# Where each half of the next weight tile is split, from step 28 on: at the step's beginning, or behind the attention operations of its first two gaps

## The chip, the cores and the metric

The kernel runs on one core of a Trainium2 chip. The metric is the time of one execution on the device in microseconds (us). Of the kernel before there are three runs, 1799.41 to 1800.14 us, with a median of 1799.8 us.

## What is computed

One layer of a hybrid backbone, in float32, for 128 context tokens and 256 latent tokens (384 rows, three row blocks of 128), with D_MODEL 2048:

```
mod = silu(cond) @ w_mod + b_mod                     # 2048 x 12288, context and latent
h   = rmsnorm(x, g0) * (1 + sc_m) + sh_m
u   = h @ w_in                                       # 2048 x 5120
m   = concat(A(u), B(u), C(u), D(u))                 # the mixers
x   = x + g_m * rmsnorm(m @ w_out, g1)               # 2048 x 2048
h   = rmsnorm(x, g2) * (1 + sc_f) + sh_f
a, g = split(h @ w_ffn_in)                           # 2048 x 11264
x   = x + g_f * rmsnorm((silu(g) * a) @ w_ffn_out, g3)   # 5632 x 2048
```

A is differential attention (4 heads, each with two softmaxes whose difference is taken), B a bidirectional recurrent unit (RG-LRU), C neighbourhood attention (4 heads, with a bias table), D grouped-query attention (4 query heads, 2 key heads). Latent tokens attend to cached context keys and their own.

## The kernel before, in words

**Weights.** Every weight is streamed once, in tiles of 128 x 2048 numbers (1 MB), through `RAW` = 6 buffers, by SyncE's queue, in the order of the list `PLAN`. Each tile of a large product is split into a high and a low part, so that three passes of a faster number format (`F32R`) give a float32 product: ScalarE copies a tile into `whi` (function `hi`, the instruction is at line 460), VectorE writes raw minus high over the raw tile as `wlo` (function `lo`, line 1224), and TensorE multiplies high by high, low activations by high, and high activations by low (lines 934, 935, 936). Each of the two split functions works in two halves of 1024 columns; its argument `bs` says which. The semaphore `w_hi` counts high halves, `w_lo` low halves. `whi` is a ring of two tiles (`RING`), so a high half of tile t+2 waits until TensorE has used that half of tile t (`w_used`).

**Steps.** The input projection is 40 steps (`IN_STEPS`) and the output projection 16 more, so `STEPS` is 56, one weight tile each. A step (`step_tile`) multiplies one tile with each of the three row blocks tb = 0, 1, 2: 12 matmuls of 512 columns for each. It takes both halves of its tile at its start: `parts = list(halves(...))` waits for both `w_lo` counts before the first matmul. Ahead of the tile, up to step 35, two tiles of the modulation product are multiplied (line 806).

**Gaps.** From step 16 on, attention is worked off between the row blocks. After row block tb of step s comes gap (s, tb) with number g = 3s + tb, and the table `GAPS` holds its operations: K and Q (transposes of keys and queries), S (scores of one unit, a head and a row block), P (transposes of its probabilities), V (product with the values). TensorE issues them (lines 1027, 1034, 1048, 1061, 1071). On ScalarE the same gap holds the copies of the transposes out of PSUM (line 592), the eviction of a finished block (491 or 628), the exponentials of an S (603), a square for mixer A's norm behind a V (655), and the splitting of finished rows of the mixers' output (`CONV`, 662). On VectorE it holds the eviction of a V (1470), the row maxima of an S (1444, 1445), the addition of a partial output block (1489), and the probabilities' weights of the S one gap earlier (1456 to 1460; for mixer A they include the difference of the softmaxes, for which the P waits). Each engine works strictly in its written order. From step 36 to 43 the pattern has a period of two steps: an even step has V (K) in gap 0, P and S in gap 1, V and Q in gap 2; an odd step has P and S in gap 0, V alone in gap 1, P and S in gap 2. Steps 44 to 50 hold mixer C, steps 29 to 35 mixer D. In steps 52 to 55 gaps 0 and 1 hold on VectorE the addition of the last partial block, on ScalarE its square (635), on TensorE a broadcast of gains (1106); VectorE also builds diagonals (1524) and multiplies finished blocks by the gains (1539).

**Where the next tile is split.** Step s prepares the tile of step s+1. ScalarE calls `hi(*step_key(s + 1))` at line 690, behind gap (s-1, 2) and ahead of gap (s, 0). VectorE calls `lo(*step_key(s + 1))` at line 1561, at the same place of its own order. So both halves are split in the first third of a step, and the operations of gaps (s, 0) and (s, 1) stand behind them in both queues.

Of the kernel before, what the change touches and what calls it, by code (L numbers as in the profile page):

```python
# [32 lines left out]
KG = 4  # L33
# [16 lines left out]
KH = KD // 2  # L50
KG2 = FK // KG
EARLY = 4
IN_STEPS = IN_N * KG
OUT_N = D // NC
OUT_KG = [1, 3, 0, 2]
STEPS = IN_STEPS + OUT_N * KG

# [12 lines left out]
def in_step(s):  # L70

    return (s % EARLY, s // EARLY) if s < EARLY * KG else (s // KG, s % KG)


def step_key(s):

    if s < IN_STEPS:
        return ("in",) + in_step(s)
    if s < STEPS:
        return ("out", s % OUT_N, OUT_KG[(s - IN_STEPS) // OUT_N])  # L80
    return ("up", 0, 0)


def mod_tiles(s):

    if s < 2:
        return 0, []
    if s < EARLY:
        return FINE + s - 2, [0, 1, 2, 3]
# [108 lines left out]
def build(nc, wst, xt_d, x_p, x_s, cdiff, cna, cgqa, c, c_ctx, lam_w, gate_w, na_rpb, qk_g, par_d, tables_d,  # L198
# [101 lines left out]
    with ExitStack() as ctx:  # L300
# [94 lines left out]
        def in_bank(s, tb):  # L395

            return (4 if s < EARLY * KG and s % 2 else 0) + tb

# [52 lines left out]
        def _(act):  # L451
# [186 lines left out]
            def gap(s, tb):  # L638

                g = TB * s + tb  # L640
                for task in GAPS[g]:
                    if task[0] in ("P", "K", "Q"):
                        t_out(task)
                if s < STEPS - OUT_N:
                    group_out(s, tb)
                for what, u in GAPS[g]:
                    if what == "S":
                        exponent(u)
                for what, u in GAPS[g]:
                    if what == "V" and UNITS[u][0] == "A":  # L650
                        a = u - A0
                        act.wait_ge(o_ev, u + 1)
                        if a >= 3:
                            act.wait_ge(ss_ok, a - 2)
                        nc.scalar.activation(junk[a % 3][:, :], q_of(u), ACT.Square, accum_out=ssA[:, a:a + 1]).then_inc(ss_ok, 1)
                if g == TB * IN_STEPS - 1:
                    act.wait_ge(st_t, 1)
                    nc.scalar.activation(rows_st[0:8, :], ps[3][0:8, 0:P], ACT.Copy).then_inc(st_cp, 1)
                if g in CONV:
                    kind, h = CONV[g]  # L660
                    act.wait_ge(cv_ps, CONV_NO[kind, h] + 1)
                    nc.scalar.activation(h_hi[:, KBASE[kind] + h, :], ps[3][:, 0:T], ACT.Copy).then_inc(cv_hi, 1)
                if s >= STEPS - OUT_N:
                    group_out(s, tb)

            for s in range(STEPS):
                i, phase = (s - EARLY * KG) // 3, (s - EARLY * KG) % 3
                lru = 0 <= i < 4
                m, kgs = mod_tiles(s)
                if s > EARLY * KG:  # L670
                    gap(s - 1, 2)
                if s == 0:
                    rows_out(2)
                    rows_out(3)
                    hi(*step_key(1), bs=(0,))
                    h_shift(2)
                    h_shift(3)
                    hi(*step_key(1), bs=(1,))
                if s == 1:
                    part_out(0)  # L680
                    part_out(1)
                if KG - 1 in kgs:
                    rows_out(m)
                if s == 3:
                    for k in range(KG, 2 * KG):
                        h_shift(k)
                if lru and phase == 0:
                    lru_in(i)
                if s:
                    hi(*step_key(s + 1))  # L690
                if s == EARLY * KG:
                    act.wait_ge(l_setup, 2)
                if s == 3:
                    part_out(2)
                    part_out(3)
                if s in (7, 11):
                    for k in range(s + 1, s + 1 + KG):
                        h_shift(k)
                if lru and phase == 1:
                    lru_gates(i)  # L700
                if lru and phase == 2:
                    lru_sqrt(i)
                if s == EARLY * KG:
                    act.wait_ge(lam_p, 1)
                    nc.scalar.activation(lamt[:, 2:4], lamt[:, 0:2], ACT.Exp).then_inc(lam_e, 1)
                    act.wait_ge(part_d, TB * EARLY * (KG - 1))
                    norm_squares(2, DK, 12, 0)
                if s == EARLY * KG + 2:
                    norm_squares(4, DQ, 0, 6)
                if s in (IN_STEPS - 2, IN_STEPS - 1):  # L710
                    act.wait_ge(w_used, used("in", IN_N - 1, 1))
                    for n in range(2 * (s % 2), 2 * (s % 2) + 2):
                        nc.scalar.activation(h_hi[:, 4 + n, :].rearrange("p (t f) -> p t f", f=P),
                                             u3(BX + n * P, P), ACT.Copy).then_inc(mb_hi, 1)
                if s >= EARLY * KG:
                    gap(s, 0)
                    gap(s, 1)

            def y_out(y, n, last):

# [486 lines left out]
        def _(dve):  # L1207
# [75 lines left out]
            def gain(k0, j, one, ks=range(KD)):  # L1283
                a, n = ks[0], len(ks)
                g = pc2[:, NG + KD * j + a:NG + KD * j + a + n].unsqueeze(2).to_broadcast([P, n, 2])
                m = modc[:, k0 + a:k0 + a + n, :]
                if one:
                    link(V.scalar_tensor_tensor(m, m, 1.0, g, ALU.add, ALU.mult))
                else:
                    link(V.tensor_tensor(m, m, g, ALU.mult))  # L1290
# [250 lines left out]
            for s in range(STEPS):  # L1541
                i, phase = (s - EARLY * KG) // 3, (s - EARLY * KG) % 3
                lru = 0 <= i < 4
                m, kgs = mod_tiles(s)
                n = s - (STEPS - OUT_N)
                if s > EARLY * KG:
                    gap(s - 1, 2)
                if n >= 0:
                    diagonal(G_M, n, 0, 2 * n + 1)
                if s in (2, 3):  # L1550
                    mod_out(m)
                    if s == 2:
                        dve.wait_ge(xr_ok, 1)
                        col_scaled(KG, KG, m).then_inc(xs_ok, 1)
                    else:
                        for k in range(KG, 2 * KG):
                            first_h(k)
                if lru and phase == 0:
                    lru_conv(i)
                if s:  # L1560
                    lo(*step_key(s + 1))
                if n > 0:
                    for tb in range(TB):
                        y1_gate(n - 1, tb)
                if KG - 1 in kgs and EARLY <= s < EARLY * KG:
                    mod_out(m)
                    if m < 10 and m % 2 == 0:
                        dve.wait_ge(xr_ok, m // 2 - 1)
                        col_scaled(KG * (m // 2 - 1), KG, m).then_inc(xs_ok, 1)
                if s == 2:  # L1570
                    softplus()
                if s in (7, 11):
                    for k in range(s + 1, s + 1 + KG):
                        first_h(k)
                if EARLY <= s < EARLY * KG:
                    part_add(s)
                if s >= EARLY * KG:
                    gap(s, 0)
                    if KG - 1 in kgs:
                        mod_out(m)  # L1580
                if lru and phase == 1:
                    lru_decay(i)
                if lru and phase == 2:
                    lru_scan(i)
                if s in (IN_STEPS - 2, IN_STEPS - 1):
                    for b in range(2 * (s % 2), 2 * (s % 2) + 2):
                        dve.wait_ge(mb_hi, b + 1)
                        V.tensor_tensor(h_lo[:, 4 + b, :].rearrange("p (t f) -> p t f", f=P), u3(BX + b * P, P),
                                        h_hi[:, 4 + b, :].rearrange("p (t f) -> p t f", f=P).bitcast(F32),
                                        ALU.subtract).then_inc(mb_lo, 1)  # L1590
                if s == IN_STEPS + 7:
                    dve.wait_ge(mod_col, len(MOD_K0))
                    gain(G_M, 1, False)
                    gain(SC_F, 2, True)
                if s >= EARLY * KG:
                    gap(s, 1)
                if -1 <= n < OUT_N - 1:
                    diagonal(G_M, n + 1, 1, 2 * n + 2)

# [378 lines left out]
```

## Time and profile before

| | |
|---|---|
| median of three runs | 1799.8 us |
| the profiled execution, its own time | 1798.27 us |
| its span in the profile | 1796.4 us |
| TensorE busy (matmuls) | 1763.2 us, 98% |
| VectorE busy | 947.0 us, 53% |
| ScalarE busy | 659.8 us, 37% |
| GpSimd busy | 125.9 us, 7% |
| HBM read | 310.52 MB |

In the profile PE is TensorE's matmuls and PEld its weight loads, DVE is VectorE, ACT ScalarE, POOL GpSimd, SPq SyncE's DMA queue. A number such as L460 is a line of the kernel. A row of the timeline gives the start, the length, the engine, the line and the operation, what it writes and reads, and in brackets how long the engine stood idle before it and what ended that. `x2` means that two such instructions were merged into one row.

Steps 28 to 54, whose preparation the change touches, run from 345.2 to 655.8 us of the span.

### The profile page before, as it was taken

The page shows a single profiled execution, that of the slowest core. Times are in us where ns is not written, and L with a number is a line of the kernel's source. Part 1 is how long each engine was busy: PE and PEld are TensorE (multiplying, and loading weights), DVE is VectorE, ACT ScalarE, POOL GpSimd, SP SyncE. Part 2 cuts the span into 40 slices and gives each one's busy share as a digit, 9 for nine tenths or more (in the row PEclk, how much of TensorE's full clock was granted, in tenths as well). Part 3 has the DMA queues.
Part 4 walks back from the last instruction along what each step waited for, and adds up shares of the span by engine and source line. Part 5 has one row for each costly group of instructions (what it writes and reads, how often), then busy time and mean ns, then how long its engine had stood idle before and what let it go on. Part 6 is the DMA issues. An engine that isn't in the chain of part 4 may idle for free.

```text
span 1796.4 us, 22651 instructions
## 1 busy us (share of the span) xinstructions
PE 1763.2 (98%) x9499; PEld 1526.4 (85%) x9499; DVE 947.0 (53%) x1276; ACT 659.8 (37%) x952; POOL 125.9 (7%) x172
## 2 busy tenths in 40 slices
PE   5999999999999999999999999999999999999998
PEld 4667666677778879999999999999999988888886
DVE  5554578633657677356656633333333455555554
ACT  3422354443464344222222222222222344454542
POOL 1001045420300010000000000000000000000000
PEclk9999999999999999999999999999999999999999
DMA  9988777775322242345454443433333333333331
GB/s 395 349 331 318 299 270 273 294 265 228 114 104 94 104 177 117 118 172 203 167 207 188 182 147 117 140 118 124 135 117 140 119 124 134 117 138 121 121 113 71
DMA packets 47046, 317.37 MB, mean 177 GB/s; under 512 B 5433, under 2 KB 7665, under 8 KB 10017
## 3 DMA queue, kind: packets, MB, share of 16 engines
q1 hardware_dynamic: 44592, 305.35, 45.4%
q0 software_dynamic: 2288, 10.56, 1.8%
q8 instruction: 75, 1.23, 0.3%
q14 instruction: 27, 0.21, 0.0%
q10 hardware_dynamic: 64, 0.02, 0.0%
HBM read 310.52 MB, written 5.39 MB: 176 GB/s over the span
## 4 chain that ended last, share of the span: by engine, by line
PE 93%; DVE 3%; DMA 2%; ACT 1%; issue 0%; POOL 0%; SPq 0%; DVEq 0%; POOLq 0%; ACTq 0%
PE ps L1158 41%; PE ps L934 7%; PE ps L936 7%; PE ps L935 7%; PE ps L828 7%; PE ps L829 7%; PE ps L827 7%; PE ps L806 3%; DMA raw<-in_weights 2%; PE ps L1048 1%; PE ps L1071 1%; DVE wlo L1224 1%; PE ps L1106 1%; PE ps L894 1%; PE ps L896 1%; PE ps L895 1%
## 5 line engine op out<-in xcount | busy, mean ns | idle before, releaser
L1224 DVE TENSOR_TENSOR wlo<-raw,whi 128x1024 fp32r<-128x1024 f32 x376 | 459.8, 1236 | 692.6 <-ACT whi L460 692.1
L460 ACT ACTIVATE whi<-raw 128x1024 fp32r<-128x1024 f32 x376 | 392.3, 1058 | 829.7 <-PE ps L1158 507.0
L1158 PE MATMUL ps<-h_hi,whi 128*128 128x384 f32 x1408 | 471.4, 335 | 0.5 <-DVE h_lo L1303 0.5
L1158 PE MATMUL ps<-h_hi,wlo 128*128 128x384 f32 x1408 | 470.4, 334 | 0.0
L1158 PE MATMUL ps<-h_lo,whi 128*128 128x384 f32 x1408 | 470.3, 334 | 0.0
L1158 PEld LDWEIGHTS ps<-h_hi,whi 128*128 128x128 f32 x1408 | 264.3, 188 | 0.7 <-issue 0.7
L1158 PEld LDWEIGHTS ps<-h_lo,whi 128*128 128x128 f32 x1408 | 264.3, 188 | 0.0
L1158 PEld LDWEIGHTS ps<-h_hi,wlo 128*128 128x128 f32 x1408 | 264.3, 188 | 0.0
L934 PE MATMUL ps<-whi,h_hi 128*128 128x512 f32 x624 | 259.8, 416 | 0.2 <-DVE wlo L1224 0.2
L936 PE MATMUL ps<-wlo,h_hi 128*128 128x512 f32 x624 | 244.5, 392 | 0.0
L935 PE MATMUL ps<-whi,h_lo 128*128 128x512 f32 x624 | 243.6, 390 | 0.0
L827 PE MATMUL ps<-whi,j_hi 128*128 128x512 f32 x516 | 204.0, 395 | 0.0
L829 PE MATMUL ps<-wlo,j_hi 128*128 128x512 f32 x516 | 200.9, 389 | 0.0
L828 PE MATMUL ps<-whi,j_lo 128*128 128x512 f32 x516 | 200.9, 389 | 0.0
L934 PEld LDWEIGHTS ps<-whi,h_hi 128*128 128x128 f32 x624 | 117.2, 188 | 54.6 <-issue 28.7
L936 PEld LDWEIGHTS ps<-wlo,h_hi 128*128 128x128 f32 x624 | 117.1, 188 | 25.9
L935 PEld LDWEIGHTS ps<-whi,h_lo 128*128 128x128 f32 x624 | 117.5, 188 | 25.1 <-issue 1.9
L828 PEld LDWEIGHTS ps<-whi,j_lo 128*128 128x128 f32 x516 | 96.9, 188 | 21.9 <-issue 1.9
L827 PEld LDWEIGHTS ps<-whi,j_hi 128*128 128x128 f32 x516 | 96.9, 188 | 21.8 <-issue 1.9
L829 PEld LDWEIGHTS ps<-wlo,j_hi 128*128 128x128 f32 x516 | 96.9, 188 | 20.1
L1635 DVE TENSOR_TENSOR j_lo<-h3T,j_hi 128x1536 fp32r<-128x1536 f32 x44 | 77.4, 1758 | 8.4 <-ACT j_hi L762 8.4
L1855 POOL TENSOR_TENSOR smalls<-smalls 128x3 f32<-128x3 f32 x2 | 0.4, 188 | 1027.0 <-ACT ps L725 998.2
(257 smaller groups left out, 1363.6 us busy)
## 6 DMA issues: line engine op xcount, KB each, us to landing
raw<-in_weights SPq DMA_DIRECT2D x278, 1024.0 KB, 4.9
raw_x<-in_weights SPq DMA_DIRECT2D x6, 1024.0 KB, 18.5
xT<-in_x_t SPq DMA_DIRECT2D x4, 768.0 KB, 7.0
out<-x_sb SPq DMA_DIRECT2D x6, 512.0 KB, 2.7
x_sb<-in_x_sample POOLq DMA_DIRECT2D x1, 2048.0 KB, 11.0
sbc<-silu_rows POOLq DMA_DIRECT2D x1, 2048.0 KB, 8.2
gw<-in_lru_gate_w SPq DMA_DIRECT2D x4, 256.0 KB, 3.3
out<-U POOLq DMA_DIRECT2D x4, 256.0 KB, 5.6
```

The lines of the kernel that those rows point to most:

```text
L460: nc.scalar.activation(whi[:, 2 * (g % RING) + b], raw_of(t)[:, HK * b:HK * b + HK].rearrange("p k n -> p (k n)"), ACT.Copy).then_inc(w_hi, 1)
L806: ins = nc.tensor.matmul(ps[mod_bank(m)][32 * kk:32 * kk + 32, :], stat[:, 2 * k:2 * k + 32], raw_of(t)[:, kk, :], start=(kg == 0), stop=( ...
L827: nc.tensor.matmul(acc, xh[:, kk + HK * b, xs], wh[:, cols], start=(k == 0), stop=False)
L828: nc.tensor.matmul(acc, xl[:, kk + HK * b, xs], wh[:, cols], start=False, stop=False)
L829: ins = nc.tensor.matmul(acc, xh[:, kk + HK * b, xs], wl[:, cols], start=False, stop=(k == k_last))
L894: nc.tensor.matmul(acc, h_hi[:, k, xs], wh[:, cols], start=(k == 0), stop=False)
L934: nc.tensor.matmul(acc, h_hi[:, k, xs], wh[:, cols], start=begin, stop=False)
L935: nc.tensor.matmul(acc, h_lo[:, k, xs], wh[:, cols], start=False, stop=False)
L936: ins = nc.tensor.matmul(acc, h_hi[:, k, xs], wl[:, cols], start=False, stop=end)
L1158: return nc.tensor.matmul(ps[bank][:, 0:T], w[:, k % KH * P:(k % KH + 1) * P], xs[:, k, :], start=first, stop=last)
L1224: V.tensor_tensor(wlo[:, 2 * SLOT[t] + b], raw_of(t)[:, HK * b:HK * b + HK].rearrange("p k n -> p (k n)"), whi[:, 2 * (g % RING) + b].bitc ...
L1635: V.tensor_tensor(j_lo[v % 2][:, :, :], h3T[:, KG * q:KG * q + KG, :], j_hi[v % 2][:, :, :].bitcast(F32), ALU.subtract).then_inc(jl, 1)
```

## The change

A constant `LATE_SPLIT` = 28 is added. For steps 28 to 54 the call that splits both halves at the step's beginning is left out on both engines. Instead ScalarE copies half 0 of the next tile behind gap (s, 0) and half 1 behind gap (s, 1); VectorE subtracts half 0 behind gap (s, 0) and half 1 behind gap (s, 1). TensorE's and SyncE's programs, GpSimd's, and step 55 (which prepares the first tile of the next phase) are as before.

```diff
--- before.py
+++ after.py
@@ -50,6 +50,7 @@
 KH = KD // 2
 KG2 = FK // KG
 EARLY = 4
+LATE_SPLIT = EARLY * KG + 12
 IN_STEPS = IN_N * KG
 OUT_N = D // NC
 OUT_KG = [1, 3, 0, 2]
@@ -686,7 +687,7 @@
                         h_shift(k)
                 if lru and phase == 0:
                     lru_in(i)
-                if s:
+                if 0 < s < LATE_SPLIT or s == STEPS - 1:
                     hi(*step_key(s + 1))
                 if s == EARLY * KG:
                     act.wait_ge(l_setup, 2)
@@ -714,7 +715,11 @@
                                              u3(BX + n * P, P), ACT.Copy).then_inc(mb_hi, 1)
                 if s >= EARLY * KG:
                     gap(s, 0)
+                    if LATE_SPLIT <= s < STEPS - 1:
+                        hi(*step_key(s + 1), bs=(0,))
                     gap(s, 1)
+                    if LATE_SPLIT <= s < STEPS - 1:
+                        hi(*step_key(s + 1), bs=(1,))
 
             def y_out(y, n, last):
 
@@ -1557,7 +1562,7 @@
                             first_h(k)
                 if lru and phase == 0:
                     lru_conv(i)
-                if s:
+                if 0 < s < LATE_SPLIT or s == STEPS - 1:
                     lo(*step_key(s + 1))
                 if n > 0:
                     for tb in range(TB):
@@ -1592,8 +1597,12 @@
                     dve.wait_ge(mod_col, len(MOD_K0))
                     gain(G_M, 1, False)
                     gain(SC_F, 2, True)
+                if LATE_SPLIT <= s < STEPS - 1:
+                    lo(*step_key(s + 1), bs=(0,))
                 if s >= EARLY * KG:
                     gap(s, 1)
+                if LATE_SPLIT <= s < STEPS - 1:
+                    lo(*step_key(s + 1), bs=(1,))
                 if -1 <= n < OUT_N - 1:
                     diagonal(G_M, n + 1, 1, 2 * n + 2)
```

## Rows read from the trace of the kernel before

**Rows 1.** The page: busy share of each engine, and the granted TensorE clock.

```profile
PE 1763.2 (98%) x9499; PEld 1526.4 (85%) x9499; DVE 947.0 (53%) x1276; ACT 659.8 (37%) x952; POOL 125.9 (7%) x172
...
PEclk9999999999999999999999999999999999999999
```

**Rows 2.** Waits of the weight loads, 345 to 656 us: total us, times, longest.

```profile
PEld ps L934 <- issue: 11.4, 20, 0.8
...
PEld ps L1061 <- DVE pb L1460: 2.2, 1, 2.2
...
PEld ps L1071 <- issue: 0.7, 1, 0.7
```

**Rows 3.** The page: costliest groups, the two that split a weight tile.

```profile
L1224 DVE TENSOR_TENSOR wlo<-raw,whi 128x1024 fp32r<-128x1024 f32 x376 | 459.8, 1236 | 692.6 <-ACT whi L460 692.1
L460 ACT ACTIVATE whi<-raw 128x1024 fp32r<-128x1024 f32 x376 | 392.3, 1058 | 829.7 <-PE ps L1158 507.0
```

**Rows 4.** Timeline of step 38 (start us, length us, engine, line, operation, count).

```profile
470.76 0.50 PE L934 MATMUL ps<-whi,h_hi 128*128 128x512 f32 x1
...
472.48 2.00 ACT L460 ACTIVATE whi<-raw 128x1024 fp32r<-128x1024 f32 x2
...
477.66 0.92 PE L1048 MATMUL ps<-kT,qT 64*128 64x384 f32 x4
...
481.10 0.20 ACT L603 ACTIVATION_READ_ACCUMULATOR pb<-ps,smalls 128x1 f32 x1
...
481.82 0.47 PE L934 MATMUL ps<-whi,h_hi 128*128 128x512 f32 x1
```

**Rows 5.** Timeline of step 39 and the start of step 40.

```profile
488.61 0.20 ACT L603 ACTIVATION_READ_ACCUMULATOR pb<-ps,smalls 128x1 f32 x1
...
489.67 0.35 DVE L1470 TENSOR_SCALAR U<-ps,smalls 128x128 f32<-128x128 f32 x1 [1.20 <-PE ps L1071]
...
490.05 0.31 ACT L655 ACTIVATE junk<-U 128x128 f32<-128x128 f32 x1 [0.46 <-DVE U L1470]
...
493.11 0.48 PE L934 MATMUL ps<-whi,h_hi 128*128 128x512 f32 x1
```

**Rows 6.** Timeline of step 37, with GpSimd's operation on the neighbourhood bias.

```profile
457.48 0.47 PE L934 MATMUL ps<-whi,h_hi 128*128 128x512 f32 x1
...
464.56 4.57 POOL L1835 TENSOR_TENSOR nabias<-nabias,tables 128x2048 f32<-128x2048 f32 x1 [3.59 <-DMA nabias<-rpb_pad]
...
465.79 3.37 DVE L1459 SCALAR_TENSOR_TENSOR smalls<-smalls 128x1 f32<-128x1 f32 x1
...
469.86 0.55 PE L1061 MATMUL ps<-par,pb 128*128 128x128 f32 x3 [1.80 <-DVE pb L1460]
```

**Rows 7.** Timeline at the end of step 47.

```profile
583.72 0.19 ACT L603 ACTIVATION_READ_ACCUMULATOR pb<-pb,smalls 128x1 f32 x1
...
584.70 0.48 PE L934 MATMUL ps<-whi,h_hi 128*128 128x512 f32 x1
```

**Rows 8.** Timeline of step 54 and the start of step 55.

```profile
645.84 0.39 PE L934 MATMUL ps<-whi,h_hi 128*128 128x512 f32 x1
...
646.04 0.69 DVE L1489 TENSOR_TENSOR y<-y,ps 128x512 f32<-128x512 f32 x1 [1.41 <-PE ps L936]
...
646.65 0.87 DVE L1524 TENSOR_SCALAR diag_b<-par,modc 128x128 f32<-128x128 f32 x4
...
650.75 1.88 DVE L1539 TENSOR_TENSOR y<-y,ps 128x512 f32<-128x512 f32 x3
...
653.26 0.63 ACT L635 ACTIVATE ysq<-y 128x512 f32<-128x512 f32 x1 [3.87 <-DVE y L1489]
...
655.82 0.39 PE L934 MATMUL ps<-whi,h_hi 128*128 128x512 f32 x1
```

**Rows 9.** Timeline of steps 29 and 30: the table load, and a tile's late landing.

```profile
361.02 1.28 ACT L603 ACT_TABLE_LOAD   x1
...
371.48 2.01 ACT L460 ACTIVATE whi<-raw 128x1024 fp32r<-128x1024 f32 x2 [4.94 <-DMA raw<-in_weights]
```

## The prediction

> **What bounds the kernel now.** I read the page first, then TensorE's waits in the stretch that is touched, then the timeline step by step. The reader is to see three things. TensorE is busy for 98% of the span [rows 1], so what delays it is paid in full and what is only moved beside it costs nothing. In the 311 us of steps 28 to 54 its weight loads wait for another engine in two places worth a name: 2.2 us ahead of a P in step 37, and 0.7 us ahead of a V in step 30 [rows 2]. And splitting a tile is now early: in step 38, which begins at 470.76, both high halves are started at 472.48, and the low ones follow within 4 us, while TensorE needs them only at 481.82 [rows 4]. So there is some 6 us of slack in front of each step's first matmul, and nearly nothing for the attention operations to gain by being served first.
>
> **The change part by part.** No instruction is added or removed. In each of 27 steps two copies of 1.06 us and two subtractions of 1.24 us [rows 3] move back in ScalarE's and VectorE's queues. TensorE's order and the DMA issues of SyncE are the same; a tile's release hangs on TensorE's progress alone. What matters is when the second low half ends, because the next step takes both halves ahead of its first matmul. I work that out for each kind of step, from its start, with every wait in each queue's order.
>
> *Even steps of mixer A (36, 38, 40, 42).* Gap 1 holds P and S. TensorE ends the scores of step 38 at 478.6, VectorE's maxima follow, and ScalarE's exponentials end at 481.3, with the next operation able to begin at 481.2 [rows 4]. This part needs no weights and stays where it is. Then come high half 1 to 482.3 and low half 1 to 483.5. TensorE wanted to begin step 39 at 481.82: it is 1.7 us late. Half 0 is no trouble in these steps, as gap 0 has only K and V. Four steps: 6.8 us.
>
> *Odd steps (37, 39, 41, 43).* Here gap 0 holds the scores. Step 39 begins at 481.82, its exponentials let ScalarE go at 488.7, that is at 6.9 [rows 5]. High half 0 ends at 7.95, low half 0 at 9.2. Only then may VectorE evict the V of gap 1, which it now does at 7.85. ScalarE's square starts 0.38 after the eviction's start [rows 5] and lets go after 0.3, at 9.9. High half 1 ends at 10.95, low half 1 at 12.2. Step 40 was due at 493.11 - 481.82 = 11.3, so it is late by 0.9, with the release 1.0. Four steps: 4.0 us.
>
> *Step 37 and GpSimd.* The row shows a VectorE operation on single columns that takes 3.37 us, from 465.79 to 469.16, while GpSimd's operation on the bias runs from 464.56 to 469.13; the P of gap 2 waits for it [rows 6]. After the change the step starts 1.7 us later, at 459.2, and at 467.2 low half 0 meets the same GpSimd operation. If it is held like that operation it ends at 470.4, the eviction and the square at 471.1, the halves of the second split at 472.2 and 473.4. Step 38 was due at 470.76 + 1.7 = 472.5: late by 0.9, as in the other odd steps. If low half 0 isn't held, step 37 loses its old stall and comes out 1.1 us ahead, not 1.0 behind. I take the held case, because the row is of the same engine and the same GpSimd operation; the free case stays in the range. The Trainium skill, "SBUF — State Buffer", section "Who interferes with whom", says that a VectorE instruction with two SBUF inputs and a GpSimd instruction that reads SBUF exclude each other for a whole instruction, the one that starts first keeping the ports; the subtraction has two SBUF inputs, and by that rule it is held and the sum stays as I make it, where without the rule it would be 2.1 us less.
>
> *Mixer C (44 to 50).* ScalarE is lighter here: one softmax for each S. Only where gap 1 ends in a masked S or a `CONV` is there little room. In step 47 the exponential ends at 583.9, then 1.06 + 1.24 and two releases bring the low half to 586.2, where the next step was due at 584.70 [rows 7]: 1.4 with the overlap of neighbouring operations. Step 46 has the same chain with a longer third gap, some 0.6. The others come out within 0.3 of their due time and I take them at nothing. Together 2.0 us.
>
> *Output steps 52 to 54.* At its start VectorE has, in step 54, an addition of 0.69, two sets of diagonals of 0.87 and three gains of 1.88 [rows 8]. Today low halves stand between them and nothing hangs on the order. After the change ScalarE's high half 0 waits for the square of gap 0, that for VectorE's addition, and that for all of this: the addition ends at 4.65 (0.3 off for overlap), the square at 5.4, high half 0 at 6.45, low half 0 at 7.75, the next addition at 8.4, its square at 9.15, high half 1 at 10.2, low half 1 at 11.45. The step lasts 655.82 - 645.84 = 9.98: late by 1.5. Steps 53 and 54 are alike; in step 52 the gains are not there yet, 0.4. Together 3.4 us. Into the tail the work left over on VectorE carries some 0.5 us.
>
> *Mixer D (28 to 35).* Ahead of their tiles these steps multiply two modulation tiles, which is slack enough in all but one: step 29 has an S in both gaps and, ahead of the first exponential, a table load of 1.28 [rows 9]; I take 0.5. Step 30 gains: its high halves now wait 4.94 us for the tile to land [rows 9] with the copy for a P queued behind them; served first, it removes the 0.7 us of [rows 2]. The bounds for both are 0 and 1.3 late, 0 and 0.9 gained.
>
> The sum is 6.8 + 4.0 + 2.0 + 3.4 + 0.5 + 0.5 - 0.7 = 16.5 us on the profiled execution's 1798.3, so 1814.8. That execution lies 1.5 us below the median of 1799.8, to which the measured time will compare: 1816.3 us, slower by 0.9%. What would hide the cost is slack between a gap 1 and the next step; each us of it that I have missed takes 1 us from each of some 14 steps. The trace doesn't show what a matmul costs behind such a wait: from nothing to 0.2 us each, which is up to 3 us.
>
> **The rivals.** (a) *Only the long chains are late.* Odd steps and output steps come out on time, since ScalarE and VectorE run on during TensorE's wait, and the even steps and mixer C remain: 6.8 + 2.0 = 8.8, 1808.6 us. For it: the odd steps miss by only 1.0 in a chain of seven links. Against it: all links are durations of rows.
>
> (b) *The other side: attention is served first and the halves still arrive.* Then both waits vanish, 0.7 + 2.2 = 2.9 us, 1796.9 us, within what can't be told from no change. If the "issue" pauses of 11.4 us [rows 2] were waits for late attention operations too, it would be up to 14 us, 1785.5. It decides at the second low half: it would have to be 1.7 us earlier in even steps. Against: the exponentials end 0.5 us ahead of the next step [rows 4], and 2.3 us of splitting must come behind them; and most of those pauses stand at the modulation tiles and recur alike whatever is queued.
>
> (c) *The clock.* The granted clock is at its upper level, 2.4 GHz, in all slices [rows 1], and a pause of 1.80 us [rows 6] didn't lower it. The change makes pauses of that size eight times in the 93 us of mixer A alone. Should it fall to 1.2 GHz for a third of the 20 steps from 36 on, whose 36 matmuls take about 8.2 us each, that is 7 x 8.2 = 57 us, 1873 us. The Trainium skill, "TensorE: Matmul & The Clock Gate", section "HAM oscillation — how this bites in real kernels", says that a loop that waits again and again can drop to the lower clock; by that rule the time would be this one, and the trace so far speaks against it.
>
> **How the numbers follow.** The forecast has 0.73, (a) 0.12, (b) 0.10, of which 0.03 faster by more than 0.2% (3.6 us, about what a measurement of this kernel can tell from no change), (c) 0.05. The range reaches down past (a), to 1807, and up to 1826: the sum with 3 us for the restarts, 2.5 for five steps of mixers C and D that miss by half a us, and 4 for more backlog on VectorE in the output steps and the tail. That leaves (b) and (c) out. Faster 0.03, same 0.07, slower 0.90.
>
> **What would show it.** New waits of TensorE at line 934 with VectorE's line 1224 as their releaser, once a step, in some 14 of the steps from 36 to 55, of 1 to 2 us each and some 16 us in all, the even steps of mixer A longer than the odd ones; step 38 about 12.8 us long in place of 11.06, step 54 about 11.5 in place of 9.98. The wait of 0.7 us in step 30 gone. The prediction is wrong if these waits come to under 8 us, if step 39 is as long as before, or if the granted clock of these steps falls.

## The result, and the profile after

| | before | after |
|---|---|---|
| median, us | 1799.97 (4 runs) | 1815.33 (4 runs, 1814.89 to 1816.76) |
| ratio | | 1.0087, 95% interval 1.0070 to 1.0105 |
| profiled execution, its span | 1798.27, 1796.4 | 1815.71, 1813.9 |
| TensorE busy | 1763.2 | 1769.3 |

The change costs 15.4 us in the medians and 17.5 us between the two profiled spans. All ratios leave out two single executions, of 3596.2 and 2528.5 us, one each in the runs of the bias operation alone and of both diffs together, far slower than the other ten of their run. The added lines move line 460 to 461, 934 to 939, 1224 to 1229 and 1460 to 1465; the operations are the same. On the page of after, TensorE's share and the granted clock look as in [rows 1]. The two splitting groups of [rows 3] have hardly changed; what is new is the idle time, behind the second bar, of the first matmul of each product.

```profile
L1229 DVE TENSOR_TENSOR wlo<-raw,whi 128x1024 fp32r<-128x1024 f32 x376 | 464.3, 1242 | 693.3 <-ACT whi L461 692.9
...
L939 PE MATMUL ps<-whi,h_hi 128*128 128x512 f32 x624 | 260.4, 417 | 12.6 <-DVE wlo L1229 12.6
```

The idle time of 12.6 us is that of the whole span. In the steps that the change touches the matmuls waited for line 1229 in 13 places, each at the start of a step, for 12.2 us in all; the weight loads, which go ahead of them, show somewhat more. These are the waits of the weight loads of the kernel after from 345 to 672 us, in the form of [rows 2]:

```profile
PEld ps L939 <- DVE wlo L1229: 15.4, 15, 1.7
...
PEld ps L1066 <- DVE pb L1465: 3.5, 4, 2.7
```

An even step, 38 and the start of 39, against [rows 4]. The reader is to see that ScalarE's high half now begins where the exponentials end, and that the first matmul of the next step waits for what comes of it.

```profile
485.54 1.05 ACT L461 ACTIVATE whi<-raw 128x1024 fp32r<-128x1024 f32 x1
...
486.63 1.23 DVE L1229 TENSOR_TENSOR wlo<-raw,whi 128x1024 fp32r<-128x1024 f32 x1 [2.25 <-ACT whi L461]
...
487.95 0.47 PE L939 MATMUL ps<-whi,h_hi 128*128 128x512 f32 x1 [1.50 <-DVE wlo L1229]
```

An odd step, 39 and the start of 40, against [rows 5]: the eviction of gap 1 is behind the first low half, and the second high half behind ScalarE's square.

```profile
494.74 1.05 ACT L461 ACTIVATE whi<-raw 128x1024 fp32r<-128x1024 f32 x1
...
495.83 1.22 DVE L1229 TENSOR_TENSOR wlo<-raw,whi 128x1024 fp32r<-128x1024 f32 x1 [1.31 <-ACT whi L461]
...
496.97 0.34 DVE L1475 TENSOR_SCALAR U<-ps,smalls 128x128 f32<-128x128 f32 x1
...
497.66 1.05 ACT L461 ACTIVATE whi<-raw 128x1024 fp32r<-128x1024 f32 x1
...
498.74 1.22 DVE L1229 TENSOR_TENSOR wlo<-raw,whi 128x1024 fp32r<-128x1024 f32 x1 [0.44 <-ACT whi L461]
...
500.06 0.47 PE L939 MATMUL ps<-whi,h_hi 128*128 128x512 f32 x1 [0.54 <-DVE wlo L1229]
```

Step 37 and what followed it, against [rows 6]. Beside GpSimd's operation on the bias the first low half takes three times its length, the P of gap 2 waits 2.28 us for what is queued behind that low half, and step 38 then waits again.

```profile
465.05 4.61 POOL L1844 TENSOR_TENSOR nabias<-nabias,tables 128x2048 f32<-128x2048 f32 x1 [4.13 <-DMA nabias<-rpb_pad]
...
467.06 3.68 DVE L1229 TENSOR_TENSOR wlo<-raw,whi 128x1024 fp32r<-128x1024 f32 x1 [2.25 <-ACT whi L461]
...
472.04 0.55 PE L1066 MATMUL ps<-par,pb 128*128 128x128 f32 x3 [2.28 <-DVE pb L1465]
...
473.74 0.77 PE L939 MATMUL ps<-whi,h_hi 128*128 128x512 f32 x1 [0.74 <-DVE wlo L1229]
```

The first matmul of step 38 takes 0.77 us. The stretches of that place show why (length, busy time with count for each engine, the granted clock as PEclk, the share and rate of the DMA engines):

```profile
470.00:474.00 4.00, 1.23 (x8) 0.90 (x9) 3.46 (x9) 1.84 (x4) 0.00 (x0) 0.92 0.70 262
474.00:478.00 4.00, 4.00 (x13) 3.17 (x14) 0.38 (x3) 1.63 (x6) 0.00 (x0) 0.66 0.00 0
```

In the same stretches the clock before was 1.00. A mean of 0.92 and 0.66 of full speed in two stretches of 4 us is some 3.4 us at TensorE's lower level, 1.2 GHz; in the next stretch it is 1.00 again.

I took the length of every step from the start of its first matmul to that of the next. The differences add up to the 17.5 us of the spans within rounding; a step from 31 on that isn't in the table changed by less than 0.07 us.

| steps | before, us | after, us | difference | foretold |
|---|---|---|---|---|
| 30 | 13.66 | 13.08 | -0.6 | -0.7 |
| 36, 40, 42 | 11.10, 12.20, 11.10 | 12.88, 13.56, 12.81 | +4.9 | +5.1 |
| 38 | 11.06 | 14.21 | +3.15, of which 1.4 the clock | +1.7 |
| 37, 39, 41, 43 | 13.28, 11.29, 11.55, 10.89 | 14.54, 12.11, 12.47, 12.10 | +4.2 | +4.0 |
| 44 to 47 | 11.12, 11.60, 11.78, 11.35 | 11.31, 11.39, 12.48, 12.87 | +2.2 | +2.0 |
| 52, 53, 54 | 9.97, 9.97, 9.98 | 10.30, 11.09, 11.08 | +2.55 | +3.4 |
| 55 and behind | | | +0.6 | +0.5 |
| 29 | 11.77 | 11.76 | 0.0 | +0.5 |
| ahead of step 29 | | | +0.5 | 0 |

The last row is nothing of the change: in the profiled executions step 29 began anywhere from 356.3 to 357.5 us, whatever the kernel. Nor need the 1.4 us of the clock be: in the experiments below it fell at this place in a kernel that splits late in steps 29 and 30 alone. Without these two, 15.6 us are left, close to the 15.4 of the medians. A step that waits grew by 0.2 to 0.3 us more than the idle time shown ahead of it (step 36: 1.77 and 1.53), in part because the row of a 512-column matmul is 0.4 us long while the next one starts after 0.23.

### The profile page after: what moved, and what is told of

The parts are those of the page before. It is cut to its first block, busy times and chain, and to the rows that moved or that the text cites. A ratio compares the mean times of both kernels' runs of the same rounds, so it can differ in the third digit from the quotient of the medians.

```text
span 1813.9 us, 22679 instructions
## 1 busy us (share of the span) xinstructions
PE 1769.3 (98%) x9499; PEld 1528.2 (84%) x9499; DVE 948.5 (52%) x1276; ACT 659.2 (36%) x952; POOL 126.0 (7%) x172
## 4 chain that ended last, share of the span: by engine, by line
PE 90%; DVE 4%; ACT 2%; DMA 1%; issue 1%; POOL 0%; SPq 0%; DVEq 0%; ACTq 0%; POOLq 0%
PE ps L1163 40%; PE ps L939 7%; PE ps L833 6%; PE ps L834 6%; PE ps L832 6%; PE ps L941 6%; PE ps L940 6%; PE ps L811 3%; DVE wlo L1229 2%; DMA raw<-in_weights 1%; ACT whi L461 1%; PE ps L1053 1%; PE ps L1076 1%; PE ps L899 1%; PE ps L901 1%
## 5 line engine op out<-in xcount | busy, mean ns | idle before, releaser
L1163 PE MATMUL ps<-h_hi,wlo 128*128 128x384 f32 x1408 | 470.4, 334 | 0.0
L939 PE MATMUL ps<-whi,h_hi 128*128 128x512 f32 x624 | 260.4, 417 | 12.6 <-DVE wlo L1229 12.6
```

The costliest lines, as they stand in the source:

```text
L939: nc.tensor.matmul(acc, h_hi[:, k, xs], wh[:, cols], start=begin, stop=False)
L1163: return nc.tensor.matmul(ps[bank][:, 0:T], w[:, k % KH * P:(k % KH + 1) * P], xs[:, k, :], start=first, stop=last)
```

## The experiments

All ten ran beside the kernel before, whose median was 1799.1 to 1799.6 in the three groups of runs. Differences by step below are to the profile of before.

**VectorE alone.** Whose queue costs?

```diff
-                if 0 < s < LATE_SPLIT or s == STEPS - 1:
+                if s:
                     hi(*step_key(s + 1))
...
-                        hi(*step_key(s + 1), bs=(0,))     # and the call for half 1
```

> Only VectorE's halves are moved behind the gaps; ScalarE copies both high halves at the step's beginning, as in the kernel before. Theory (the second low half is late because its high half stands behind ScalarE's exponentials and squares of gap 1): the chain loses its longest link. In an even step of mixer A VectorE's maxima end at 9.3 us of the step and the low half at 10.6, due at 11.1; in an odd step it ends near 10.3, due at 11.3; in step 54 near 8.5, due at 9.98. So no new wait for line 1229, and 1799.5 to 1800.5 us, within 0.1% of before. Step 30 keeps its old wait, as ScalarE's copy of probabilities stands behind high halves that wait for a tile. Rival (VectorE's own order is what costs, the gap operations standing ahead of the subtractions): steps 36 to 43 keep at least half of their loss and the time stays above 1807.

Measured: 1801.8 us, ratio 1.0013 (1.0004 to 1.0022). Steps 36, 39, 41, 42 and 43, and 52 to 54 are as before. That is 1.3 us above what the theory allowed, and there are new waits for the low half. Three places I had not foreseen: step 37 +0.5, step 40 +0.9, steps 46 and 47 +0.6 together; and the clock fell in step 38 of the profiled execution (+1.6). In step 40 the second low half stands behind the low part of a finished row (line 1515), which waits for ScalarE behind the exponentials, and step 41 waits for that low half:

```profile
506.46 0.56 DVE L1515 TENSOR_TENSOR h_lo<-ps,h_hi 128x384 fp32r<-128x384 f32 x1 [1.68 <-ACT h_hi L663]
...
506.94 1.21 DVE L1225 TENSOR_TENSOR wlo<-raw,whi 128x1024 fp32r<-128x1024 f32 x1
...
508.25 0.47 PE L935 MATMUL ps<-whi,h_hi 128*128 128x512 f32 x1 [0.63 <-DVE wlo L1225]
```

One foretold row was wrong too: step 30 gained its 0.6 here as well (13.08), though ScalarE's order is that of before. So that gain is VectorE's: the eviction of gap 0's V, at 374.85 us in the trace of before, stood behind low halves whose tile landed late; here it starts at 371.92. The rival falls: VectorE's order by itself costs 1.9 us beside the clock, less the 0.6 of step 30; that is far from half of the loss.

**Half 0 early.** Both engines split half 0 at the step's beginning, half 1 behind gap 1. The diff shows the first of these on ScalarE; VectorE's `lo` is changed in the same way, and the calls for half 0 behind gap 0 are gone.

```diff
-                if 0 < s < LATE_SPLIT or s == STEPS - 1:
-                    hi(*step_key(s + 1))
+                if s:
+                    hi(*step_key(s + 1), bs=(0,) if LATE_SPLIT <= s < STEPS - 1 else (0, 1))
```

> Half 0 is split at the step's beginning on both engines, only half 1 behind gap (s, 1). Theory (in odd and output steps half 0's subtraction stands in front of the gap 1 operations and pushes them back): the even steps 36, 38, 40, 42 keep their loss of 1.4 to 1.8 us each, 6.5 in all; the odd steps come out on time, steps 53 and 54 late by no more than 0.5; step 37 has its low half 0 ahead of GpSimd's operation, so no pause of 5 us and no fall of the clock in step 38. Mixer C keeps 2.2. In all 1809 to 1810 us. Rival (only half 1's place matters): odd and output steps lose as after the whole change, and the time is 1813 to 1816.

Measured: 1807.49 us, 1.0045 (1.0033 to 1.0058). Even steps +1.8, +1.75, +1.35, +1.8, the same as in the change; the odd ones 39, 41, 43 within 0.04 of before; 37 -0.3; 46 and 47 +2.2; 52 +0.3, 53 and 54 +0.4 each; no fall of the clock. The rival, that odd and output steps lose as much as in the whole change, is refuted. The theory's steps are right, its total 1.5 us or more too high, of which 0.9 is that I had left out step 30's -0.6 and step 37's -0.3.

**Both halves behind gap 0.** Against the kernel after, on both engines:

```diff
-                        hi(*step_key(s + 1), bs=(0,))
+                        hi(*step_key(s + 1), bs=(0, 1))
                     gap(s, 1)
-                    if LATE_SPLIT <= s < STEPS - 1:
-                        hi(*step_key(s + 1), bs=(1,))
...
-                    lo(*step_key(s + 1), bs=(0,))
+                    lo(*step_key(s + 1), bs=(0, 1))
...
-                if LATE_SPLIT <= s < STEPS - 1:
-                    lo(*step_key(s + 1), bs=(1,))
```

> Both halves are split behind gap (s, 0), nothing behind gap (s, 1). Theory (the order of each queue decides, worked out chain by chain): even steps and output steps come out on time, at most 0.3 late each; in odd steps the second low half is ready at 10.3 of 11.3, but now the eviction and the weights of the V and S stand behind it, so the P of gap 2 waits for them about 1.1 us: three steps, 3.3 us, with line 1465 and not 1229 as releaser. In step 37 both halves are held by GpSimd's operation: P comes 3 us later than before the change, and the clock falls for a while as it did. In all 1806 to 1809 us. Rival (any splitting behind attention costs what it cost in the whole change): 1813 to 1816. Rival (only the distance to the next step matters): 1799.5 to 1801.

Measured: 1808.5 us, 1.0046 (1.0034 to 1.0059). Steps 36 and 42, 46 to 54 as before; 39, 41 and 43 +1.18, +1.25, +1.18 with line 1463 as releaser (the foretold 1465 under this kernel's numbering); 37 +2.7, and the clock fell in 38. Both rivals are refuted. Step 40 has +0.95, nearly as in the first experiment, but by another wait: here both low halves stand ahead of the row maxima, and it is the transposes of gap 2 that wait 0.93 us for the finished row's low part. The wait has changed its place: in this kernel's step 39 the two low halves are in time, and the P of gap 2 comes late.

```profile
494.29 2.36 DVE L1227 TENSOR_TENSOR wlo<-raw,whi 128x1024 fp32r<-128x1024 f32 x2 [1.31 <-ACT whi L461]
...
497.28 0.62 DVE L1463 SCALAR_TENSOR_TENSOR pb<-pb,smalls,pb 128x384 f32<-128x384 f32 x1
...
497.95 0.55 PE L1064 MATMUL ps<-par,pb 128*128 128x128 f32 x3 [0.97 <-DVE pb L1463]
```

**High halves behind gap 0, low halves as in the change.** Takes one link out of the chain, the high half behind gap 1.

```diff
-                        hi(*step_key(s + 1), bs=(0,))
+                        hi(*step_key(s + 1), bs=(0, 1))
                     gap(s, 1)
-                    if LATE_SPLIT <= s < STEPS - 1:
-                        hi(*step_key(s + 1), bs=(1,))
```

> ScalarE copies both high halves behind gap (s, 0); VectorE subtracts half 0 behind gap (s, 0) and half 1 behind gap (s, 1), as in the change. Only high half 1 is taken out from behind gap 1's exponentials and squares. Theory (that is the link that makes the second low half late): even steps lose 0 to 0.1 in place of 1.4 to 1.8, step 46 and 47 at most 0.4, steps 53 and 54 nothing, since their low half 1 ends at 9.7 of 9.98. Odd steps lose 0.6 in place of 0.8 to 1.2: there the eviction and weights of the gap stand between. Step 37 is held by GpSimd as before, 1.0 to 1.3, and the clock may fall, 1.4. Step 40 keeps 0.9, from a finished row's low part. In all 1804 to 1806 us. Rival (the low halves' own place costs as much): above 1810.

Measured: 1804.46 us, 1.0029 (1.0018 to 1.0039). Step 36 0.0, 42 -0.05, 46 and 47 +0.6, 52 to 54 0.0; 39, 41, 43 +0.3, +0.4, +0.7; 37 +1.6, 40 +0.85, and 1.6 in step 38 with the clock. The time and the even steps are as the theory has them, and the rival (above 1810) falls. Of the 15 us, 10 hang on ScalarE's second high half standing behind the gap's exponentials and squares.

**The bias operation in four.** The whole change, with GpSimd's operation cut by head.

```diff
-            G.tensor_tensor(nb, nb, tables[:, 0:64]....to_broadcast([P, 32, GRID_W]), ALU.add).then_inc(bias_ok, 1)
+            for h in range(4):
+                nb = nabias[:, h].rearrange("p q i w -> p (q i) w")
+                G.tensor_tensor(nb, nb, tables[:, 0:64]....to_broadcast([P, 8, GRID_W]), ALU.add).then_inc(bias_ok, 1)
...
-                        dve.wait_ge(bias_ok, 1)
+                        dve.wait_ge(bias_ok, 4)
```

> The whole change, and GpSimd's one operation on the neighbourhood bias (4.6 us) is made as four, one for each head, with the first user waiting for all four. Theory (in step 37 low half 0 is held for 2.4 us by that one operation, and the pause of TensorE that follows lets the clock fall in step 38): step 37 shrinks from 14.5 to about 12.7 us and step 38 from 14.2 to 12.8, 1812 us in all, 3.2 less than after the change. Rival (the clock falls because of the series of pauses, not this one): step 38 keeps its 14.2 or another step has it, 1813.7. Rival (VectorE is held by each of the four in turn, as long in total): no gain, 1815.3.

Measured: 1813.54 us, 1.0080 (1.0067 to 1.0094). Step 37 takes 13.18, step 38 12.81, no stretch at the lower clock; all other steps are those of the change. The low half is still held, but for 1.0 us and not 2.5. Of GpSimd's four operations the first three take 1.27 to 1.29 us each; the fourth, which starts while the low half is at work, takes 2.25:

```profile
464.38 5.98 POOL L1845 TENSOR_TENSOR nabias<-nabias,tables 128x512 f32<-128x512 f32 x4 [3.57 <-DMA nabias<-rpb_pad]
...
466.98 2.25 DVE L1229 TENSOR_TENSOR wlo<-raw,whi 128x1024 fp32r<-128x1024 f32 x1 [2.25 <-ACT whi L461]
```

The profiled span is 3.1 us shorter than that of after, which had the fall of the clock. By medians, each against its own runs of before, 14.2 us are left of 15.4, and the median lies 1.5 us above the 1812 foretold; the two intervals overlap. So the steps of the trace show the gain of 1.4 us in step 37, the medians don't separate it, and the theory's 3.2 holds at most for an execution with the fall.

**Filling the pause.** Small matmuls ahead of the P of step 37's gap 2, first 20, then 10.

```diff
+                if u == A0 + 2:
+                    pe.wait_ge(mod_col, len(MOD_K0))
+                    for _ in range(20):     # 10 in the second
+                        nc.tensor.matmul(ps[3][:, NC - P:NC], ones[:, :], ident[:, :], start=True, stop=True, skip_group_check=True)
```

> The whole change, with 20 small matmuls whose result nobody reads (128 columns each, about 2.3 us in all) issued in gap 2 of step 37, ahead of the transposes that wait there. They fill a pause of 2.9 us and move nothing else. Theory (1.4 us of step 38's loss is TensorE at 1.2 GHz after that pause): step 37 stays at 14.5 us, step 38 takes 12.8 in place of 14.2, the granted clock is 1.00 from 470 to 482 us, and the time is 1813.5 to 1814 and scatters less than after the change. Rival (step 38 is long because VectorE or ScalarE is behind): step 38 stays at 14.2 with the clock at 1.00.

Measured: 1815.95 us, 1.0094 (1.0080 to 1.0108). Step 38 takes 12.88 at a clock of 1.00, but step 37 15.7: a float32 matmul is two rows of the trace, the filling took 4.62 us and pushed the P back. So the run was mis-sized and its total says nothing on the cost of the clock.

> The whole change with 10 small matmuls in gap 2 of step 37. The run with 20 of them showed each as two passes and 4.6 us in all, 1.7 us more than the pause holds; 10 take 2.3 us and end before the probabilities are there. Theory (1.4 us of step 38 is the lower clock): step 37 stays at 14.5, step 38 takes 12.85, no stretch at 1.2 GHz in the profiled execution, 1813.5 to 1814.3 us. Rival (what's left of the pause, some 0.6 us and 0.7 ahead of step 38, is still enough for the clock to fall): step 38 at 14.2.

Measured: 1814.79 us, 1.0085 (1.0071 to 1.0098). Step 37 14.62, step 38 12.82, and the clock stays up, with the wait of 0.74 ahead of step 38 still there:

```profile
470.09 2.39 PE L1063 MATMUL ps<-par,ones 128*128 128x128 f32 x20
...
474.30 0.47 PE L939 MATMUL ps<-whi,h_hi 128*128 128x512 f32 x1 [0.74 <-DVE wlo L1233]
```

The 1.4 us of step 38 is the clock, then, and not a backlog: the same wait stands ahead of the step, and the step is shorter by that much. That the filling is what kept the clock up is not shown by one profiled execution. The four runs lie within 0.9 us of each other. The median is only some 0.5 below that of after, and above the 1813.5 to 1814.3 foretold. That would fit a fall that some executions have and others haven't, but how often the kernel after has it was not counted.

**Towards a better kernel.** Step 30's gain alone, the bias operation alone, and both.

The first confines the change to steps 29 and 30:

```diff
-LATE_SPLIT = EARLY * KG + 12
+late = lambda s: s in (29, 30)
...
-                if 0 < s < LATE_SPLIT or s == STEPS - 1:
+                if s and not late(s):
...
-                    if LATE_SPLIT <= s < STEPS - 1:
+                    if late(s):
```

> The change in steps 29 and 30 alone; all other steps split at their beginning. Theory (each step's loss and gain is its own): step 30 takes 13.1 in place of 13.7 and all other steps are as before, 0.6 us less than before, which is at the edge of what can be measured. Rival (the gain of step 30 is used up behind it): no difference in the span of steps 29 to 56.

Measured: 1798.5 us, 0.9995 (0.9986 to 1.0004): not to be told from before. In the trace step 30 takes 13.08, all others as before but for 38, where the clock fell in that execution (+1.5), behind a pause of 1.75 us (1.80 in the trace of before, where it stayed up) that is there without the change too.

The second is the kernel before with the bias diff shown above and nothing else.

> The kernel before, with GpSimd's operation on the bias made as four. The second low half isn't in play here. Theory (in step 37 TensorE waits 2.0 us only because a column operation of VectorE is held by GpSimd's whole operation): step 37 takes 11.3 to 12.2 us in place of 13.3, and the time is 1797.2 to 1798.6. Rival (held four times over): no change.

Measured: 1797.24 us, 0.9990 (0.9981 to 0.9999). Step 37 takes 11.26, all of its 2.0 us gone, which is the lower end that I had given. The difference of the softmaxes (line 1460) is now what is held, 1.62 us in place of 0.62, but it begins early enough.

```profile
465.90 5.34 POOL L1836 TENSOR_TENSOR nabias<-nabias,tables 128x512 f32<-128x512 f32 x4 [3.78 <-DMA nabias<-rpb_pad]
...
467.24 1.62 DVE L1460 SCALAR_TENSOR_TENSOR pb<-pb,smalls,pb 128x384 f32<-128x384 f32 x1
...
469.03 0.49 PE L1061 MATMUL ps<-par,pb 128*128 128x128 f32 x3
```

The third has both of these diffs.

> The change in steps 29 and 30 alone, and the bias operation made as four: the version to which the runs so far point. Theory: both gains add, 0.6 in step 30 and 1.1 to 2.0 in step 37, 1796.7 to 1798 us, faster than both kernels. Rival: the gain of step 37 lets attention run into the next wait and is given back by step 40.

Measured: 1797.18 us, 0.9989 (0.9980 to 0.9998). Steps 30 and 37 both gain, 2.6 us by the table of steps, and nothing is given back by step 55. It is faster than both kernels, than the one before by only 0.1% and an interval that ends just below 1; against the bias operation alone the medians don't separate it.

## Why the prediction was right

The forecast was 1816.3 us, the median is 1815.33. The large terms were right in mechanism and size: the sum was 16.5 us, and the steps from 29 on give 15.6 without the clock. Two terms were too large, the output steps by 0.85 and step 29 by 0.5; a few too small ones offset part of that. In the profiled execution the fall of the clock (1.4 us) and the later start of step 29 (0.5), for which the sum had nothing, bring the difference to 17.5 us. The second is chance; whether the change makes the first more frequent is not shown. One of the signs by which the prediction called itself wrong did come: the granted clock fell, in one step.

- *The second low half ends behind the next step's start.* Right, and shown: taken out of ScalarE's gap 1, the high half stops costing in steps 36 and 42 and in the output steps. The waits number 13, of 0.2 to 1.5 us, where some 14 of 1 to 2 us were foretold. (The slack of 6 us was read rightly, but in step 38 of before the low halves ended at 475.93, 5.2 us into the step: just under half of the step, and not the first third that the description of the kernel gives.)
- *Even steps.* Foretold 1.7 each and 12.8 us for step 38; they are 1.8, 1.4, 1.7, and 12.8 wherever the clock didn't fall.
- *Odd steps.* 1.0 each foretold, 0.8 to 1.3 found. Shown to hang on half 0: with half 0 early they are on time. Rival (a), that they would come out on time anyway, is refuted.
- *Step 37.* That the low half would be held was right, its end within 0.4 us (467.2 to 470.4 foretold, 467.06 to 470.74 in the trace). By the Trainium skill's rule ("SBUF — State Buffer", section "Who interferes with whom") the two instructions exclude each other for a whole instruction; the trace agrees, 3.68 us for an operation of 1.22, ending 1.1 behind GpSimd's end at 469.66. The step is late by 1.26 in place of 0.9. The difference stands in that end: GpSimd's operation, which waits for a DMA, began at 465.05 and not at 464.56 as before. What follows took 2.9 us where I had 3.0.
- *The clock.* I gave it a rival with a third of 20 steps, 57 us, and nothing in the sum. It fell once, and cost 1.4 us in the profiled execution. That a pause can lower the clock was right, the price forty times too large. By the rule of the Trainium skill ("TensorE: Matmul & The Clock Gate", section "HAM oscillation — how this bites in real kernels") waits that recur can each drop the clock if they are long enough; this trace has one fall, at its longest pause, and the other 12 waits for line 1229, of up to 1.5 us, left the clock at 1.00. Nor is the fall peculiar to the change, as the run of steps 29 and 30 alone has it too.
- *Output steps.* 3.4 foretold, 2.55 found. The chain was right link by link. In step 54 its second low half ends 11.0 us after the start and not 11.45: an operation begins up to 0.1 us before the one ahead of it on its engine ends (low half 0 ends at 669.04, the addition behind it begins at 668.95), and I took off 0.3 in all.
- *Step 29.* 0.5 foretold, 0 found: the table load doesn't delay the first exponential. ScalarE is idle at the step's beginning once the splitting has gone, and loads the table ahead of its wait:

```profile
357.54 1.28 ACT L604 ACT_TABLE_LOAD   x1
...
361.03 0.37 ACT L604 ACTIVATE pb<-ps,smalls 128x128 f32<-128x128 f32 x1 [2.20 <-DVE smalls L1450]
```

- *Step 30.* -0.7 foretold, -0.6 found, but for a wrong reason: I named ScalarE's copy behind the high halves, and moving VectorE alone gives all of it, with ScalarE's copy still behind both high halves.
- *Rival (b), the gain.* What attention won by being first was the 0.6 us of step 30; the wait in step 37 grew. The "issue" pauses were no hidden waits: 11.4 us before, 10.6 after.

A place that I missed is step 40, where VectorE's low part of a finished row (line 1514 before) stands ahead of the second low half and itself waits for ScalarE. With VectorE alone moved this costs 0.9 us; in the change the same wait is 1.36 in all. I had counted step 40 with the even steps at 1.7.

## What to carry to other kernels

Before work is moved behind other work in an in-order queue, find the latest moment at which its result is taken and walk the chain of every engine to it: here 6 us of slack became up to 1.7 us too few, ahead of the engine that bounds the kernel, in 13 of the 27 steps. Work whose result is taken at the next step's first instruction belongs ahead of operations that wait on another engine's chain, however much these look like the urgent ones. And ask what a moved operation will stand beside: one GpSimd operation of 4.6 us cost the kernel before 2.0 us in one step, more than the change costs in any step but for the clock, and cutting it in four was the only thing here by which the time fell measurably, by 1.9 us or 0.1%.

## What the runs showed of the hardware

- In the twelve profiled executions, one for each kernel, TensorE's clock fell around the start of step 38 in five, each time for some 3.4 us, behind pauses in step 37 of 4.44 us (both halves behind gap 0), 3.13 (high halves behind gap 0), 2.28 (the change), 1.98 (VectorE alone) and 1.75 (steps 29 and 30 alone). It stayed up behind 1.80 (before), 1.42 and 1.26, behind every wait of 1.53, and where the pause was filled or gone. So nearly the same pause, 1.75 and 1.80, went either way. A fall cost 1.4 to 1.6 us.
- GpSimd's operation takes 4.56 to 4.61 us whole. In four parts each takes 1.27 to 1.29 us, but 1.59 or 2.25 where VectorE's held operation gets its turn, 5.34 or 5.98 in all: both engines pay, but the hold on VectorE's low half goes from 2.5 us to 1.0.
